# Smaller batches of moves in the transfer queue, and one of four weight sums made by adding transfers, in a stack of nine fp32 transformer stages

## The chip, the cores and the metric

One core of a Trainium2 chip runs the whole program. The metric is the device time of one execution in microseconds (us), the median of several runs. A profiled execution gives the rows that are read here; its own time and its span are given below.

## The reference, cut to what matters

The input is x, 512 tokens by 1024 features, in fp32. Nine stages follow each other: FFN stages 1, 3, 4, 6, 7 and 9, and mixers 2 (pooling and latent attention), 5 (gated convolution) and 8 (Fourier mixing and grouped attention). The change is in the FFN stages alone:

```python
def rms_norm(x, g):
    y = xf * lax.rsqrt(jnp.mean(xf * xf, axis=-1, keepdims=True) + NORM_EPS)
    return (y * g).astype(x.dtype)

def swiglu(x, w_gate, w_up, w_down):
    return (jax.nn.silu(x @ w_gate) * (x @ w_up)) @ w_down

x = x + 0.5 * swiglu(rms_norm(x, ffn_norm), w_gate, w_up, w_down)
```

w_gate and w_up are 1024 x 2816 (2752 in stages 7 and 9), w_down is 2816 x 1024.

## The kernel before, in words

**Precision.** Every fp32 operand is split in a high part (rounded to fp32r, by ACT) and a low part (the rest, by DVE). A product is three matmuls (L556 low by high, L558, L560 high by high; `mm3`). A weight block of 128 x 1024 numbers comes from HBM into one of eight `raw` slots (issued by SP, L2529), is split by ACT into `wh` (L1146, `high`) and by DVE into `wl` (L1614, `low`), and is then a *unit* that TensorE uses (12 matmuls in a group, 24 in the down projection's first part). The split buffers are a ring of four: ACT may write unit n when TensorE is through with unit n - 4. ACT and DVE work three units ahead of TensorE (two in the down projection).

**The group.** An FFN stage treats the first 2560 hidden columns in five groups of 512 (g = 0 to 4). The two products with w_gate and w_up, halved in the inner dimension and in the tokens, are a 2 x 2 block product, and it is made with seven block products instead of eight (a Strassen form). It needs four sums of activation blocks (Sf 0 to 3, made once in a stage) and four sums of weight blocks in every group, each in two halves kh = 0 and 1: t1 from B12 and B11, t2 from B22 and t1, t3 from t2 and B11, t4 from B21 and t2. So a group has 14 units, in this order: B11 (product A), t1 (E), t2 (B), t3 (D), t4 (B2), B21 (A2), B22 (E2), each twice. t1 overwrites the raw slot of B12, t3 that of B11; t2 and t4 stand in the two buffers `part`. All eight sums are made by DVE (L1601, `add`), in group 0 just before the split of their unit and in groups 1 to 4 two units earlier (`sums_before`).

TensorE leaves products A, B, D and E in PSUM; DVE combines them through U2, U3 and H (L1624: `U2`, `C22`, `C21`, `last_sum`), ACT applies silu (L1219, L1226), DVE gates (L1627).

**Turning H.** The hidden block comes out with tokens on the partitions and is needed with hidden columns there. DVE turns 32 x 32 pieces (L1717, `turn_squares`), into rows of H that are not used yet (`squares(m)`; for m = 3 into `squares3`), and sixteen transfers of 64 KB inside SBUF, issued by SP (L2536, `move_blocks`), put the 32-row pieces in their places. Groups 0 to 3 (m = 0 to 3) go that way; group 4 is turned by TensorE (L680). The last columns behind 2560 (256, or 192 in stages 7 and 9) stand in `Hrest` and are batch m = 4: turned by `turn_rest_squares` (L1724) in group 1, into rows 14 and 15 of H. H, once moved, is split into `Hh` (ACT, L1177) and `Hl` (DVE, L1624) for the down projection.

**The order of SP's queue.** SP works strictly in order. It issues the weight loads, each of which waits until its raw slot has been split for the last time (L2522), and the moves, which wait for the squares. Where the moves stand is worked out when the program is built (L2540 to L2546): a batch (q, g, u) is put ahead of the first load whose slot is released at unit u of group g or later, the whole batch of sixteen in one piece. Batches 0 and 4 are placed at units 7 and 8 of group 1, 1 and 2 at unit 7 of groups 2 and 3, and 3 at unit 10 of group 4. In stage 1 this puts batch 0 ahead of load 24 and batch 4 ahead of load 25; loads 21 to 28 are the eight of group 2, and load 25 (B22, kh = 0) is the first that t2 needs. Batch 3 stands ahead of the second down load in stage 1 and ahead of the first in the other stages, whose raw slots come free later.

POOL has little to do: in an FFN stage one power for the norm (`norm`, L2373).

Of the kernel before, what the change touches and what calls it, by code (L numbers as in the profile page):

```python
# [160 lines left out]
def plan(stream):  # L161


    loads, units, release = [], [], []
    begins = {}
    holder, ring = {}, {}
    free_at = {r: -1.0 for r in range(N_RAW)}
    sums = {}

    def load(chunk, allowed, last):  # L170
        r = min(allowed, key=lambda slot: (free_at[slot], slot))
        loads.append(Load(*chunk, r, holder.get(r)))
        holder[r], free_at[r] = len(loads) - 1, last
        release.append(last)
        return len(loads) - 1

    def unit(width, nk, allowed, ahead, source, total=None):
        r = min(allowed, key=lambda slot: (ring.get(slot, -1), slot))
        units.append(Unit(width, nk, r, ring.get(r), ahead, source, total))
        ring[r] = len(units) - 1  # L180

    for c in stream:
        u = len(units)
        if not isinstance(c[2], dict):
            n = load(c, PLAIN if u >= len(FIRST) else range(N_RAW), u)
            unit(c[1], c[2], PLAIN, 2, ("raw", n))
            continue
        s, first, blocks = c
        begins.setdefault(s, []).append(u)
        if first and s in AFTER_MIXER:  # L190
            for r in range(len(PLAIN), N_RAW):
                holder[r], free_at[r] = ("end", s - 1), u - 4.0
        raw = {}
        for name, kh in (sorted(LOADS, key=lambda part: UNITS.index(part[0]) if part[0] in UNITS[0:1] else LAST_USE[part[0]])
                         if first else LOADS):
            last = u + LAST_USE[name] + kh + (2 if first and name == "B12" else 0)
            raw[name, kh] = load(blocks[name, kh], range(N_RAW), last)
        for name in UNITS:
            for kh in range(2):
                b11, b12, b21, b22 = (("raw", raw[b, kh]) for b in ("B11", "B12", "B21", "B22"))  # L200
                part = ("part", kh)
                source, total = {
                    "t1": (b12, (b12, b11, ALU.subtract)), "t2": (part, (b22, b12, ALU.subtract)),
                    "t3": (b11, (part, b11, ALU.subtract)), "t4": (part, (b21, part, ALU.subtract)),
                    "B11": (b11, None), "B22": (b22, None), "B21": (b21, None)}[name]
                if total:
                    sums.setdefault(len(units) - (1 if first else 2), []).append(len(units))
                unit(512, 2, range(N_RING), 3, source, total)
    return loads, units, release, sums, begins

# [39 lines left out]
def build(nc, a, out):  # L250
    ctx = ExitStack()
    with ctx:
# [17 lines left out]
        par_in, gain_in, out_in = Event(sem("par_in")), Event(sem("gain_in")), Event(sem("out_in"))  # L270
        x_in = [Event(sem(f"x_in{t}")) for t in range(KT)]
        turned_in = [Event(sem(f"turned_in{q}")) for q in range(5)]

# [16 lines left out]
        sq_at = -(-(place[0] - 128) // 256) * 256 + 128  # L290
        sq = [sb(f"sq{i}", [128, T], F) for i in range(2)]
        acc = [sb(f"acc{i}", [128, T], F) for i in range(2)]
        diag_at = place[0]
# [15 lines left out]

        ident = col("ident", 0, 128)  # L310
        loads, units, release, sums_before, begins = plan(weight_stream(a))


# [11 lines left out]
        Sl = [at(f"Sl{j}", [128, 4, 256], R, 49152 + 8192 * j) for j in range(4)]  # L325
        part = [at(f"part{j}", [128, CAP], F, 77824 + 4096 * j) for j in range(2)]
        wh.append(at("wh3", [128, CAP], R, 86016))
        wl.append(at("wl3", [128, CAP], R, 90112))
# [8 lines left out]

        squares3 = at("squares3", [128, 4, 4, 128], F, 45056 + 16384)

        def squares(q):  # L340

            return squares3[:, :, :, :] if q == 3 else H[:, 4 * q + 8:4 * q + 12, :, :]

        def block_moves(s, m):

            spans = [slice(32 * i, 32 * i + 32) for i in range(4)]
            for j in spans:
                for i in spans:
                    if m < 4:
                        yield H[j, 4 * m:4 * m + 4, :, i], squares(m)[i, :, :, j]  # L350
                    else:
                        whole = (FFN[s][0] - GROUPED - j.start + 127) // 128
                        yield H[j, 20:20 + whole, :, i], H[i, 14:14 + whole, :, j]

# [774 lines left out]
        def scalar_program(e, w):  # L1129
# [3 lines left out]
            def high():  # L1133
# [4 lines left out]
                split[0] += 1  # L1138
                if units[n].sum:
                    w.wait_ge(dve, ("t", n))  # L1140
                else:
                    i = units[n].source[1]
                    w.wait_ge(raw_in[loads[i].slot], ("w", i))
# [442 lines left out]
        def vector_program(e, w):  # L1586
# [122 lines left out]
            def turn_squares(s, m, *ks):  # L1709

                w.wait_ge(dve, ("h", s, m))
                if m == 1:
                    w.wait_ge(turned_in[4], ("turned", s, 4))
                if m == 3:
                    w.wait_ge(mm, ("E", s, 4))
                for k in ks:
                    e.transpose(squares(m)[:, k, :, :], H[:, 4 * m + k, :, :]).then_inc(dve.up(("squares", s, m)), 1)  # L1717

            def turn_rest_squares(s, n):

                w.wait_ge(dve, ("h", s, 5))
                for k, cols in ((14, 128), (15, n - 128)):
                    at0 = 128 * (k - 14)
                    e.transpose(H[:, k, :, 0:cols], Hrest[:, :, at0:at0 + cols]).then_inc(dve.up(("squares", s, 4)), 1)  # L1724

# [18 lines left out]
            def last_sum(s, g):  # L1744
                x = pairs[pairs_of(s)[3]]
                w.wait_ge(mm, ("E2", s, g))
                tt(hidden(g, 0), blocks(x), blocks(U2), ALU.add, ("C12", s, g), ("read", ("E2", s, g)))

# [6 lines left out]
            def ffn(s):  # L1755
# [4 lines left out]
                w.wait_ge(act, ("second half", s))  # L1760
                tt(Sf[2][:, :, :], Qf[1][:, :, :], Sf[2][:, :, :], ALU.add, ("S1", s))
                use()
# [11 lines left out]
                for g in range(5):  # L1774
                    for u in range(14):
# [6 lines left out]
                        if u == 8:  # L1782
# [4 lines left out]
                            w.wait_ge(dve, ("U3", s, g))  # L1787
                            for m in {2: (0,), 3: (1, 4), 4: (2,)}.get(g, ()):
                                w.wait_ge(turned_in[m], ("turned", s, m))
                            tt(hidden(g, 2), blocks(x), blocks(U3), ALU.add, ("C22", s, g), ("read", ("E", s, g)))  # L1790
                        if u == 10:
# [12 lines left out]
                        if u == 3 and g == 0:  # L1804
                            w.wait_ge(act, ("other half", s))
                            w.wait_ge(dve, ("N2", s))
                            tt(Sf[3][:, :, :], Qf[2][:, :, :], Sf[1][:, :, :], ALU.add, ("S4", s))
                        if u == 5 and g == 0:
# [4 lines left out]
                        if u in (5, 6) and g == 4:  # L1813
                            turn_squares(s, 3, 2 * u - 10, 2 * u - 9)
                        if u == 4 and g == 1:
                            turn_rest_squares(s, f - GROUPED)
# [552 lines left out]
        def gpsimd_program(e, w):  # L2369
            pool.n = 0  # L2370

            def tt(dst, a, b, op, *names):
# [6 lines left out]
            def inverse_root(dst, src, shape, name, source):  # L2379
# [6 lines left out]
                w.wait_ge(pool, "half")  # L2386
                tt(dst, src, h, ALU.pow, name)

            def norm(s):
# [117 lines left out]
            for s in range(1, 10):  # L2507
                {2: mixer_mla, 5: mixer_conv, 8: mixer_fnet}.get(s, norm)(s)
                pool.also(("end", s))
# [5 lines left out]
        def sync_program(e, w):  # L2515
# [16 lines left out]

            def move_blocks(s, m):
                w.wait_ge(dve, ("squares", s, m))
                for dst, src in block_moves(s, m):
                    e.dma_start(dst, src).then_inc(turned_in[m].sem, 16)  # L2536
                    turned_in[m].n += 16
                turned_in[m].also(("turned", s, m))

            moves_before = {}  # L2540
            for s in FFN:
                for q, g, u in ((0, 1, 7), (4, 1, 8), (1, 2, 7), (2, 3, 7), (3, 4, 10)):
                    u += begins[s][g]
                    later = (n for n, load in enumerate(loads) if load.before is not None and (
                        load.before == ("end", s) if not isinstance(load.before, int) else release[load.before] >= u))
                    moves_before.setdefault(next(later, len(loads)), []).append((u, s, q))  # L2546

# [18 lines left out]
            e.dma_start(par[:, :], a["par"]).then_inc(par_in.sem, 16)  # L2566
            for n in range(13, len(loads) + 1):
                for _, s, q in sorted(moves_before.get(n, ())):
                    move_blocks(s, q)
                if n < len(loads):  # L2570
                    fetch(n)
            for part, (q0, q1) in enumerate(HALVES):
# [120 lines left out]
```

## Time and profile before

| | |
|---|---|
| median of 3 runs | 2636.38 us (2634.23 to 2637.41) |
| profiled execution | 2630.94 us |
| its span | 2629.1 us |
| TensorE (PE) busy | 2553.9 us, 97% |
| VectorE (DVE) busy | 1928.6 us, 73% |
| ScalarE (ACT) busy | 1173.5 us, 45% |
| GpSimd (POOL) busy | 136.5 us, 5% |
| mean granted TensorE clock | 0.992 |
| transfers on queue q1, share of 16 DMA engines | 37.0% |

Times in the rows count from the span's start. "Idle before" is the time that an instruction's engine stood still ahead of it, with what ended that. SPq are transfers that SP issues: the time there is the issuing, not the transfer.

### The profile page before, as it was taken

To read this page: it belongs to the slowest core of one execution; us is meant where nothing else is said; L and a number is where in the kernel's file an instruction comes from. 1 tells how busy PE (TensorE), PEld (TensorE's weight loads), DVE (VectorE), ACT (ScalarE), POOL (GpSimd) and SP (SyncE) were. 2 spreads that over 40 slices of the span, in tenths; PEclk is the share of its full clock that TensorE was granted. 3 is DMA by queue.
4 is the path that set the end of the run, shared out by engine and by line. 5 is a ranking of instruction groups with operands and counts; after the bars stand their busy time and mean duration, and the time that the engine had idled before them with its cause. 6 is when DMAs were issued, how large, how long until landed. Compare 5 with 4: busy or idle time off the path is not lost.

```text
span 2629.1 us, 31692 instructions
## 1 busy us (share of the span) xinstructions
PE 2553.9 (97%) x11743; PEld 2116.6 (81%) x11743; DVE 1928.6 (73%) x2371; ACT 1173.5 (45%) x1611; POOL 136.5 (5%) x133
## 2 busy tenths in 40 slices
PE   8999999999999999999999999999999999999998
PEld 6788888877878887788888877888787888877787
DVE  7898358888983498854556988449985479798843
ACT  6445226664443444432225544335444337644431
POOL 0000004500000000000000000000000044100000
PEclk9999999999999999999999999999999999999999
DMA  5553332134533345433333454243533321244422
GB/s 178 132 144 85 95 89 79 33 121 128 136 92 94 119 108 141 112 97 97 96 96 114 116 144 111 87 134 98 150 94 107 96 87 41 88 114 136 116 89 81
DMA packets 448761, 280.92 MB, mean 107 GB/s; under 512 B 235744, under 2 KB 383968, under 8 KB 448608
## 3 DMA queue, kind: packets, MB, share of 16 engines
q1 hardware_dynamic: 448608, 278.89, 37.0%
q8 instruction: 95, 1.56, 0.2%
q14 instruction: 58, 0.48, 0.1%
HBM read 248.68 MB, written 2.10 MB: 95 GB/s over the span
## 4 chain that ended last, share of the span: by engine, by line
PE 70%; DVE 14%; SPq 6%; issue 5%; ACT 3%; DMA 2%; DVEq 0%; POOLq 0%; POOL 0%; ACTq 0%
PE pair L556 23%; PE pair L558 22%; PE pair L560 22%; SPq L2536 5%; DVE wl L1614 5%; ACT wh L1146 1%; DMA raw<-in_ffn_w_up 1%; DMA raw<-in_ffn_w_down 1%; DVE part L1601 1%; DVE H L1717 1%; DVE U L1624 1%; PE pair L780 1%; DVE raw L1601 1%; DVE H L1627 1%; DVE squares L1717 1%
## 5 line engine op out<-in xcount | busy, mean ns | idle before, releaser
L1614 DVE TENSOR_TENSOR wl<-raw,wh 128x1024 fp32r<-128x1024 f32 (+2 forms) x547 | 647.0, 1188 | 445.0 <-ACT wh L1146 442.4
L1146 ACT ACTIVATE wh<-raw 128x1024 fp32r<-128x1024 f32 (+2 forms) x547 | 562.7, 1030 | 823.5 <-PE pair L560 749.0
L556 PE MATMUL pair<-Hh,wl 128*128 128x512 f32 (+1 forms) x1061 | 413.6, 390 | 16.7 <-DVE Hl L1624 15.7
L558 PE MATMUL pair<-Hl,wh 128*128 128x512 f32 (+1 forms) x1061 | 414.6, 391 | 0.0
L560 PE MATMUL pair<-Hh,wh 128*128 128x512 f32 (+1 forms) x1061 | 412.2, 388 | 0.0
L556 PE MATMUL pair<-wh,Sl 128*128 128x512 f32 x960 | 379.4, 395 | 25.7 <-DVE H L1624 17.7
L556 PE MATMUL pair<-wh,Xl 128*128 128x512 f32 (+2 forms) x976 | 376.3, 386 | 16.6 <-DVE wl L1614 7.0
L558 PE MATMUL pair<-wl,Sh 128*128 128x512 f32 x960 | 377.3, 393 | 0.0
L560 PE MATMUL pair<-wh,Sh 128*128 128x512 f32 x960 | 377.0, 393 | 0.0
L558 PE MATMUL pair<-wl,Xh 128*128 128x512 f32 (+2 forms) x976 | 374.1, 383 | 0.0
L560 PE MATMUL pair<-wh,Xh 128*128 128x512 f32 (+2 forms) x976 | 374.0, 383 | 0.0
L556 PEld LDWEIGHTS pair<-Hh,wl 128*128 128x128 f32 x1061 | 200.4, 189 | 60.4 <-ACT Hh L1177 17.7
L556 PEld LDWEIGHTS pair<-wh,Sl 128*128 128x128 f32 x960 | 182.5, 190 | 72.4 <-DVE H L1624 20.2
L558 PEld LDWEIGHTS pair<-Hl,wh 128*128 128x128 f32 x1061 | 200.5, 189 | 41.7
L560 PEld LDWEIGHTS pair<-Hh,wh 128*128 128x128 f32 x1061 | 200.7, 189 | 40.2
L556 PEld LDWEIGHTS pair<-wh,Xl 128*128 128x128 f32 x976 | 184.0, 189 | 55.9 <-DVE U L1624 8.8
L1146 ACT ACTIVATE wh<-part 128x1024 fp32r<-128x1024 f32 x120 | 127.4, 1062 | 225.3 <-DVE part L1601 131.7
L560 PEld LDWEIGHTS pair<-wh,Sh 128*128 128x128 f32 x960 | 182.5, 190 | 38.5
L558 PEld LDWEIGHTS pair<-wl,Sh 128*128 128x128 f32 x960 | 182.4, 190 | 37.5
L560 PEld LDWEIGHTS pair<-wh,Xh 128*128 128x128 f32 x976 | 184.1, 189 | 34.9
L558 PEld LDWEIGHTS pair<-wl,Xh 128*128 128x128 f32 x976 | 184.1, 189 | 33.9
L556 PE MATMUL pair<-Xh,wl 128*128 128x512 f32 (+1 forms) x432 | 170.9, 396 | 2.2 <-DVE Xl L1624 1.6
(325 smaller groups left out, 3287.5 us busy)
## 6 DMA issues: line engine op xcount, KB each, us to landing
raw<-in_ffn_w_gate SPq DMA_DIRECT2D x120, 512.0 KB, 4.9
raw<-in_ffn_w_up SPq DMA_DIRECT2D x120, 512.0 KB, 4.3
raw<-in_ffn_w_down SPq DMA_DIRECT2D x114, 512.0 KB, 3.5
H<-H SPq DMA_DIRECT2D x288, 64.0 KB, 2.1
raw<-in_c_w_in SPq DMA_DIRECT2D x24, 512.0 KB, 3.8
H<-squares SPq DMA_DIRECT2D x96, 64.0 KB, 2.1
raw<-in_w_in SPq DMA_DIRECT2D x10, 512.0 KB, 3.9
raw<-in_a_w_in SPq DMA_DIRECT2D x8, 512.0 KB, 3.8
```

The source lines that it names most:

```text
L556: e.matmul(o, ll, rh, start=start, stop=False, skip_group_check=again)
L558: e.matmul(o, lh, rl, start=False, stop=False, skip_group_check=again)
L560: i = e.matmul(o, lh, rh, start=False, stop=stop, skip_group_check=again)
L780: e.transpose(bank[0:rows, t * 128:(t + 1) * 128], src, ident).then_inc(mm.up(name), 1)
L1146: e.activation(part_of(n, wh), source_of(n), ACT.Copy).then_inc(whi.up(("w", n)), 1)
L1601: e.tensor_tensor(half_of(units[n].source), half_of(a), half_of(b), op).then_inc(dve.up(("t", n)), 1)
L1614: e.tensor_tensor(part_of(n, wl), source_of(n), part_of(n, wh).bitcast(F), ALU.subtract).then_inc(wlo.up(("w", n)), 1)
L1624: e.tensor_tensor(dst, a, b, op).then_inc(dve.up(*names), 1)
L1627: e.scalar_tensor_tensor(dst, a, scalar, b, op0, op1).then_inc(dve.up(*names), 1)
L1717: e.transpose(squares(m)[:, k, :, :], H[:, 4 * m + k, :, :]).then_inc(dve.up(("squares", s, m)), 1)
L2536: e.dma_start(dst, src).then_inc(turned_in[m].sem, 16)
```

## The change

Three things are changed, all in the FFN stages.

1. SP's moves of batches 0, 1 and 2 are issued in two eights, each ahead of a load: batch g - 1 ahead of the fifth load of group g + 1 and ahead of the first load behind that group's eight. Batches 3 and 4 are one sequence of 32 moves, of which 12, 2, 2, 2, 4, 4 and 6 stand ahead of the first seven down loads.
2. The last columns (batch 4) are turned in group 4, at u = 9, into a place of their own (`squares4`, over `acc`), not in group 1 into rows of H.
3. The signs in the scheme are changed so that t4 = B21 + t2 (t1 = B12 + B11, t2 = B22 + t1; S1, S4, C12 and C22 change their sign to match). DVE's instruction for t4 goes, sixty in all. In its place POOL issues a transfer from the raw slot of B21 into `part` that adds to what stands there (`accum_op`), 512 KB each. It waits for the raw block, for both splits of t2 (unit n - 4) and for t3's sum (unit n - 2). ACT's split of t4 waits for the transfer.

```diff
@@ -186,7 +186,7 @@
         s, first, blocks = c
-        begins.setdefault(s, []).append(u)
+        group_loads.setdefault(s, []).append(len(loads))
         if first and s in AFTER_MIXER:
@@ -200,13 +200,15 @@
                 source, total = {
-                    "t1": (b12, (b12, b11, ALU.subtract)), "t2": (part, (b22, b12, ALU.subtract)),
-                    "t3": (b11, (part, b11, ALU.subtract)), "t4": (part, (b21, part, ALU.subtract)),
+                    "t1": (b12, (b12, b11, ALU.add)), "t2": (part, (b22, b12, ALU.add)),
+                    "t3": (b11, (part, b11, ALU.subtract)), "t4": (part, (b21, part, None)),
                     "B11": (b11, None), "B22": (b22, None), "B21": (b21, None)}[name]
-                if total:
+                if name == "t4":
+                    adds.setdefault(s, []).append(len(units))
+                elif total:
                     sums.setdefault(len(units) - (1 if first else 2), []).append(len(units))
                 unit(512, 2, range(N_RING), 3, source, total)
-    return loads, units, release, sums, begins
+    return loads, units, release, sums, adds, group_loads
@@ -336,10 +341,11 @@
         squares3 = at("squares3", [128, 4, 4, 128], F, 45056 + 16384)
-
-        def squares(q):
-
-            return squares3[:, :, :, :] if q == 3 else H[:, 4 * q + 8:4 * q + 12, :, :]
+        squares4 = nc.alloc_sbuf_tensor_at("squares4", [128, 2, 4, 128], F, offset=acc_at)
+
+        def squares(m):
+
+            return {3: squares3, 4: squares4}[m][:, :, :, :] if m > 2 else H[:, 4 * m + 8:4 * m + 12, :, :]
@@ -350,7 +356,7 @@
                         whole = (FFN[s][0] - GROUPED - j.start + 127) // 128
-                        yield H[j, 20:20 + whole, :, i], H[i, 14:14 + whole, :, j]
+                        yield H[j, 20:20 + whole, :, i], squares4[i, 0:whole, :, j]
@@ -1136,7 +1142,9 @@
                 split[0] += 1
-                if units[n].sum:
+                if units[n].sum and units[n].sum[2] is None:
+                    w.wait_ge(added[n % 2], ("t", n))
+                elif units[n].sum:
                     w.wait_ge(dve, ("t", n))
@@ -1709,8 +1717,6 @@
                 w.wait_ge(dve, ("h", s, m))
-                if m == 1:
-                    w.wait_ge(turned_in[4], ("turned", s, 4))
                 if m == 3:
@@ -1719,9 +1725,9 @@
                 w.wait_ge(dve, ("h", s, 5))
-                for k, cols in ((14, 128), (15, n - 128)):
-                    at0 = 128 * (k - 14)
-                    e.transpose(H[:, k, :, 0:cols], Hrest[:, :, at0:at0 + cols]).then_inc(dve.up(("squares", s, 4)), 1)
+                for k, cols in ((0, 128), (1, n - 128)):
+                    e.transpose(squares4[:, k, :, 0:cols], Hrest[:, :, 128 * k:128 * k + cols]).then_inc(
+                        dve.up(("squares", s, 4)), 1)
@@ -1785,9 +1791,9 @@
                             w.wait_ge(dve, ("U3", s, g))
-                            for m in {2: (0,), 3: (1, 4), 4: (2,)}.get(g, ()):
+                            for m in {2: (0,), 3: (1,), 4: (2,)}.get(g, ()):
                                 w.wait_ge(turned_in[m], ("turned", s, m))
-                            tt(hidden(g, 2), blocks(x), blocks(U3), ALU.add, ("C22", s, g), ("read", ("E", s, g)))
+                            tt(hidden(g, 2), blocks(x), blocks(U3), ALU.subtract, ("C22", s, g), ("read", ("E", s, g)))
                         if u == 10:
@@ -1812,7 +1818,7 @@
                             turn_squares(s, 3, 2 * u - 10, 2 * u - 9)
-                        if u == 4 and g == 1:
+                        if u == 9 and g == 4:
                             turn_rest_squares(s, f - GROUPED)
@@ -2385,6 +2393,22 @@
                 tt(dst, src, h, ALU.pow, name)
+
+            def add_weights(n):
+
+                (_, b21), (_, kh), _ = units[n].sum
+                w.wait_ge(raw_in[loads[b21].slot], ("w", b21))
+                w.wait_ge(whi, ("w", n - 4))
+                w.wait_ge(wlo, ("w", n - 4))
+                w.wait_ge(dve, ("t", n - 2))
+                e.dma_start(totals[kh][:, :], raw[loads[b21].slot][:, :], accum_op=ALU.add).then_inc(added[n % 2].sem, 16)
+                added[n % 2].n += 16
+                added[n % 2].also(("t", n))
+
+            def ffn(s):
+                norm(s)
+                for n in adds[s]:
+                    add_weights(n)
@@ -2505,7 +2529,7 @@
             for s in range(1, 10):
-                {2: mixer_mla, 5: mixer_conv, 8: mixer_fnet}.get(s, norm)(s)
+                {2: mixer_mla, 5: mixer_conv, 8: mixer_fnet}.get(s, ffn)(s)
                 pool.also(("end", s))
@@ -2530,20 +2554,28 @@
-            def move_blocks(s, m):
+            def moves(s, m):
+
                 w.wait_ge(dve, ("squares", s, m))
                     turned_in[m].n += 16
-                turned_in[m].also(("turned", s, m))
+                    turned_in[m].also(("turned", s, m))
+                    yield
+
+            def last_moves(s):
+                yield from moves(s, 3)
+                yield from moves(s, 4)
             for s in FFN:
-                for q, g, u in ((0, 1, 7), (4, 1, 8), (1, 2, 7), (2, 3, 7), (3, 4, 10)):
-                    u += begins[s][g]
-                    later = (n for n, load in enumerate(loads) if load.before is not None and (
-                        load.before == ("end", s) if not isinstance(load.before, int) else release[load.before] >= u))
-                    moves_before.setdefault(next(later, len(loads)), []).append((u, s, q))
+                for g in (1, 2, 3):
+                    batch = moves(s, g - 1)
+                    for n in (4, 8):
+                        moves_before.setdefault(group_loads[s][g + 1] + n, []).append((batch, 8))
+                batch = last_moves(s)
+                for n, count in enumerate((12, 2, 2, 2, 4, 4, 6)):
+                    moves_before.setdefault(group_loads[s][4] + 8 + n, []).append((batch, count))
@@ -2564,11 +2596,11 @@
             e.dma_start(par[:, :], a["par"]).then_inc(par_in.sem, 16)
-            for n in range(13, len(loads) + 1):
-                for _, s, q in sorted(moves_before.get(n, ())):
-                    move_blocks(s, q)
-                if n < len(loads):
-                    fetch(n)
+            for n in range(13, len(loads)):
+                for batch, count in moves_before.get(n, ()):
+                    for _ in range(count):
+                        next(batch)
+                fetch(n)
             for part, (q0, q1) in enumerate(HALVES):
```

Left out are the places where a name is set up or passed on, and three more of the changed signs.

## Rows read from the trace of the kernel before

**Rows 1.** The page, part 1: busy us, share, instructions.
```profile
PE 2553.9 (97%) x11743; PEld 2116.6 (81%) x11743; DVE 1928.6 (73%) x2371; ACT 1173.5 (45%) x1611; POOL 136.5 (5%) x133
```

**Rows 2.** TensorE's waits: us in total, times, longest us.
```profile
PE pair L556 <- DVE H L1624: 17.7, 6, 4.7
PE pair L556 <- DVE Hl L1624: 15.7, 5, 4.2
PE pair L556 <- DVE wl L1614: 15.1, 17, 7.0
PE pair L556 <- DVE U L1624: 5.4, 4, 1.4
```

**Rows 3.** Timeline of TensorE, stage 3, group 2: start us, us, [idle before].
```profile
673.85 0.39 PE L556 MATMUL pair<-wh,Xl 128*128 128x512 f32 x1
674.07 0.39 PE L558 MATMUL pair<-wl,Xh 128*128 128x512 f32 x1
```

**Rows 4.** Timeline of SP's queue, stage 1, group 1.
```profile
93.08 12.05 SPq L2536 DMA_DIRECT2D H<-H  x16
...
105.85 11.94 SPq L2536 DMA_DIRECT2D H<-H  x16
117.89 1.05 SPq L2529 DMA_DIRECT2D raw<-in_ffn_w_up  x2
```

**Rows 5.** Timeline of DVE, the same stretch.
```profile
91.75 1.30 DVE L1717 STREAM_TRANSPOSE H<-H 128x512 f32<-128x512 f32 x2
...
100.02 1.22 DVE L1614 TENSOR_TENSOR wl<-raw,wh 128x1024 fp32r<-128x1024 f32 x1
...
122.21 1.22 DVE L1601 TENSOR_TENSOR part<-raw,raw 128x1024 f32<-128x1024 f32 x1 [7.78 <-DMA raw<-in_ffn_w_up]
```

**Rows 6.** Timeline of TensorE at the start of group 2, stage 1.
```profile
125.76 0.79 PE L556 MATMUL pair<-wh,Sl 128*128 128x512 f32 x1 [4.70 <-DVE H L1624]
```

**Rows 7.** Timeline of SP's queue, end of stage 3's groups.
```profile
749.12 11.97 SPq L2536 DMA_DIRECT2D H<-squares  x16
761.20 37.70 SPq L2529 DMA_DIRECT2D raw<-in_ffn_w_down  x10
```

**Rows 8.** Timeline of ACT, the same stretch.
```profile
765.53 1.06 ACT L1146 ACTIVATE wh<-raw 128x1024 fp32r<-128x1024 f32 x1 [7.29 <-DMA raw<-in_ffn_w_down]
...
767.64 1.05 ACT L1146 ACTIVATE wh<-raw 128x1024 fp32r<-128x1024 f32 x1
```

**Rows 9.** Timeline of TensorE, stage 3: group 0, and the down projection's start.
```profile
591.87 0.50 PE L556 MATMUL pair<-wh,Xl 128*128 128x512 f32 x1 [1.32 <-DVE U L1624]
...
770.70 0.61 PE L556 MATMUL pair<-Hh,wl 128*128 128x512 f32 x1 [4.21 <-DVE Hl L1624]
```

**Rows 10.** Windows: PE, PEld, DVE, ACT, POOL busy (count), PE clock, DMA share, GB/s.
```profile
125.70:129.70 4.00, 3.94 (x10) 3.17 (x11) 3.86 (x6) 1.06 (x1) 0.00 (x0) 0.57 0.53 139
...
2380.40:2384.40 4.00, 3.93 (x12) 3.19 (x13) 3.86 (x6) 1.06 (x1) 0.00 (x0) 0.69 0.60 142
...
591.80:595.80 4.00, 3.93 (x17) 3.27 (x18) 3.97 (x5) 0.81 (x1) 0.00 (x0) 1.00 0.13 15
...
770.70:774.70 4.00, 4.00 (x11) 3.17 (x12) 4.00 (x6) 2.57 (x5) 0.00 (x0) 0.57 0.56 171
...
2494.60:2498.60 4.00, 3.90 (x10) 3.15 (x11) 4.00 (x6) 2.68 (x5) 0.00 (x0) 0.57 0.54 181
```

**Rows 11.** The page, part 6: transfers, KB each, us from issue to landing.
```profile
raw<-in_ffn_w_gate SPq DMA_DIRECT2D x120, 512.0 KB, 4.9
...
H<-H SPq DMA_DIRECT2D x288, 64.0 KB, 2.1
```

**Rows 12.** Groups of DVE: count | busy us, mean ns | idle before.
```profile
L1601 DVE TENSOR_TENSOR part<-raw,part 128x1024 f32<-128x1024 f32 x60 | 73.4, 1224 | 4.4
```

**Rows 13.** Timeline of DVE, stage 3, group 0.
```profile
577.79 1.23 DVE L1601 TENSOR_TENSOR raw<-part,raw 128x1024 f32<-128x1024 f32 x1
```

**Rows 14.** Timeline of DVE, stage 3, group 2.
```profile
660.03 1.22 DVE L1614 TENSOR_TENSOR wl<-part,wh 128x1024 fp32r<-128x1024 f32 x1
```

More of the change, by code:

```diff
@@ L164, in plan @@
     loads, units, release = [], [], []
-    begins = {}
+    group_loads = {}
     holder, ring = {}, {}
     free_at = {r: -1.0 for r in range(N_RAW)}
-    sums = {}
+    sums, adds = {}, {}
     def load(chunk, allowed, last):
@@ L271, in build @@
         x_in = [Event(sem(f"x_in{t}")) for t in range(KT)]
+        added = [Event(sem(f"added{i}")) for i in range(2)]
         turned_in = [Event(sem(f"turned_in{q}")) for q in range(5)]
@@ L291, in build @@
         sq = [sb(f"sq{i}", [128, T], F) for i in range(2)]
+        acc_at = -(-(place[0] - 128) // 256) * 256 + 128
         acc = [sb(f"acc{i}", [128, T], F) for i in range(2)]
@@ L310, in build @@
         ident = col("ident", 0, 128)
-        loads, units, release, sums_before, begins = plan(weight_stream(a))
+        loads, units, release, sums_before, adds, group_loads = plan(weight_stream(a))
         stage_at = -(-(stage_base - 128) // 256) * 256 + 128
@@ L326, in build @@
         part = [at(f"part{j}", [128, CAP], F, 77824 + 4096 * j) for j in range(2)]
+        totals = part
         wh.append(at("wh3", [128, CAP], R, 86016))
@@ L1746, in last_sum @@
                 w.wait_ge(mm, ("E2", s, g))
-                tt(hidden(g, 0), blocks(x), blocks(U2), ALU.add, ("C12", s, g), ("read", ("E2", s, g)))
+                tt(hidden(g, 0), blocks(x), blocks(U2), ALU.subtract, ("C12", s, g), ("read", ("E2", s, g)))
             def hidden(g, first):
@@ L1760, in ffn @@
                 w.wait_ge(act, ("second half", s))
-                tt(Sf[2][:, :, :], Qf[1][:, :, :], Sf[2][:, :, :], ALU.add, ("S1", s))
+                tt(Sf[2][:, :, :], Qf[1][:, :, :], Sf[2][:, :, :], ALU.subtract, ("S1", s))
                 use()
@@ L1806, in ffn @@
                             w.wait_ge(dve, ("N2", s))
-                            tt(Sf[3][:, :, :], Qf[2][:, :, :], Sf[1][:, :, :], ALU.add, ("S4", s))
+                            tt(Sf[3][:, :, :], Qf[2][:, :, :], Sf[1][:, :, :], ALU.subtract, ("S4", s))
                         if u == 5 and g == 0:
@@ L2370, in gpsimd_program @@
             pool.n = 0
+            for event in added:
+                event.n = 0
             def tt(dst, a, b, op, *names):
```

## The prediction, made before the result was known

> **What bounds the kernel now.** I read the page first, for the shares: TensorE is busy for 97% of the span [rows 1], so only the stretches in which it stands still can be won. The view of waits gives these by what ended them [rows 2]: 17.7 us in six waits for DVE's H, 15.7 us in five for Hl, 15.1 us in 17 for wl (one of 7.0 us at the start), 5.4 us in four for U. Then I followed each kind back through the timelines. Matmuls start 0.22 to 0.23 us apart and are drawn 0.39 us long [rows 3], so a wait costs 0.16 us more than its printed idle time.
>
> The first kind stands at the start of group 2 of every FFN stage. In stage 1 SP issues sixteen moves in 12.05 us, one load, then sixteen more in 11.94 us, and only at 117.89 us the next two loads [rows 4]. DVE has stood still for 7.78 us when the first of them has landed, and makes its sum at 122.21 us [rows 5]. TensorE gets its buffer (the H wait) after 4.70 us [rows 6]. The second kind stands at the start of the down projection: SP issues sixteen moves in 11.97 us and only then, at 761.20 us, the first down loads [rows 7]; ACT splits the first at 765.53 us after 7.29 us of waiting for it [rows 8]; TensorE waits 4.21 us for Hl [rows 9]. The engine that sets these stalls is SP's queue.
>
> **The clock is part of the price.** After the stall at 125.7 us the granted clock over 4 us is 0.57, after that at 2380.4 us 0.69; these are the first and the last of six stalls of the first kind, and all six have such a dip (I take the mean of both, 0.63). With levels 2.4 and 1.2 GHz, a window of 4 us at mean clock c loses 4(1 - c): 1.72 and 1.24 us. Of the five Hl stalls three have one, the first and the last of them at 1.72 us [rows 10].
>
> **Part 1: moves in eights (gain 30 us).** Removed: both blocks of sixteen ahead of the loads of group 2. The batch of the last columns leaves group 1 altogether, and the other batch is split, eight moves, four loads, eight moves. Moves take 12.05/16 = 0.75 us each [rows 4], so eight hold SP for 6.0 us. In stage 1 the squares are turned by 93.05 us (two transposes from 91.75 us) and the load that DVE later misses has its slot free at 101.24 us, when the split that began at 100.02 us ends [rows 5]. In the new order SP issues the load before it, then eight moves, done by about 102 us, then this load, which lands some 4.9 us later [rows 11], at 107 us. DVE wanted it at 122.21 - 7.78 = 114.4 us: 7 us of cover. The second eight stand behind three further loads, which have their slots by then. So the stall goes: 17.7 + 6 x 0.16 = 18.7 us; the dips, six at a mean of 1.48, 8.9 us; and the six short wl waits that follow some 15 us later, where DVE is still catching up. The 16 wl waits other than the longest hold 8.1 us [rows 2], so 0.5 + 0.16 each, 4 us. Together 31.6; I take 30. The bounds are 15 (half of it comes back as shorter waits) and 32. What is late next is nothing that I can find: later groups already have one batch of sixteen ahead of loads and no stall.
>
> **Part 2: last group (gain 17 us).** The last columns are turned in group 4 (two transposes, 1.3 us like those of [rows 5]; DVE waits 7 us for the down load there, which covers them). SP issues twelve moves ahead of the first down load, not sixteen; then 2, 2, 2, 4, 4 and 6 between the loads. Twelve of 11.97/16 = 0.75 us are four fewer: the first down load is 3.0 us earlier in stage 3 [rows 7]. The blocks of the other stages last 10.68 to 11.32 us, so 2.7 to 2.8 us there. The second load comes 0.56 + 1.5 us behind the first, at 760.3 us instead of 761.8, and lands at about 764.6 us, if it takes the 4.3 us of the first (761.20 to 765.53). ACT needs it behind its first split and two silus (765.53 to 767.64 us in [rows 8], 3 us earlier in the new order, 764.6 us). So it is just in time; the third load, at 762.3 us, is level with before, and its values are wanted later. The waits shrink by 2.7 to 3.0 us in five stages: 13.9 us, which leaves 1.4 us in stage 3 and next to nothing in three. The dips behind three of them (1.72 + 1.24 + 1.72, the middle one in stage 6) are 4.7 us; a wait of 1.32 us elsewhere is followed by a clock of 1.00 [rows 9, 10]. In all 18.6 us; I take 17. Stage 1 is its own case: its first down load came before the moves and now comes behind twelve, at 228 us, which costs its 1.1 us wait nothing either way. Lower bound 5 us: the pairs of moves between loads give the gain back on the second load.
>
> **Part 3: sixty sums leave DVE (gain 7 us).** 60 instructions of 1.224 us are 73.4 us of DVE [rows 12], but where DVE waits for ACT anyway this buys nothing. It buys where DVE is the bound: in group 0. There U2 is done 2 sums (2.3 us) late, and TensorE waits 1.32 us for it in stage 3 [rows 9]. The four U waits are 5.4 + 4 x 0.16 = 6.0 us, and in stages 1 and 9 a wl wait behind the first sum goes (0.6 + 0.16 each): 7.5 us; I take 7. Other bound 0, if the add comes no earlier than the sum did. The changed signs alter no instruction's size.
>
> **Part 4: sixty adding transfers (price 0).** Behind POOL's waits stands only the next add: its own work in an FFN stage is one small power at the start. Who waits is ACT's split, then DVE's. The room: in group 0 of stage 3 the third sum starts at 577.79 us and is done 1.22 us later [rows 13], so the first add can start at 579.0. TensorE is ready for the product at 591.87 - 1.32 - 0.16 = 590.4 us [rows 9], and a split of 1.06 on ACT and 1.22 on DVE takes 2.4 us with hand-over. So the transfer has 590.4 - 2.4 - 579.0 = 9.0 us, its twin (third sum done 3.5 us later, product 2.7 us later) 8.2 us. In group 2 the last reader of the buffer starts at 660.03 us and takes 1.22, and the product starts at 673.85 us: 673.85 - 2.4 - 661.25 = 10.2 us [rows 3, 14]. The trace has no transfer from POOL and none that adds. The nearest rows are a 64 KB move inside SBUF, 2.1 us to landing, and a 512 KB load, 4.9 us [rows 11]. The ends I take are 2.1 us and 9.8 us (two passes of 4.9, as it must read two operands). I take 6: one such pass and a microsecond for POOL. At 6 us nothing waits; at 9.8 us group 0 loses 0.8 + 0.8 us in six stages, 10 us with ACT's own delays counted not at all. Sixty transfers of 4.9 us on the sixteen queues add under 300 us of a resource that is 37% busy; I give nothing for it, since the loads now have 7 us of cover.
>
> The Trainium skill speaks both ways here. Its page DMA: Bandwidth & Descriptors, "Anatomy of one DMA", fits 2.0 us + bytes/436e3 for a transfer issued from GpSimd: an estimate of 3.2 us for 512 KB, and the sum would stay. Its page SBUF, "A bandwidth-pool intuition that's wrong", tells of such a transfer at 3.1 us instead of 0.62 beside a DVE copy, because GpSimd can't write its descriptors. Estimated by that the add would be 8.5 us, and the sum 2 us less; no run here shows it yet.
>
> **Sum.** 30 + 17 + 7 - 0 = 54 us. The profiled execution took 2630.9 us (span 2629.1), so 2577 of its kind; the median of the three runs is 2636.4, 5.4 above it, and my time goes by that: 2582 us.
>
> **Rivals.**
> (a) Forecast, all stalls of the first kind gone, those of the second cut: 2574 to 2598 us. Chance 0.62.
> (b) The last group gives nothing: the down projection starts as late because the second and third load stand behind pairs of moves, or the wait passes to ACT. The exact fit above (764.6 against 764.6 us) speaks for it, the four moves fewer against. 2636 - 30 - 7 = 2599 us. Chance 0.13.
> (c) The adds land at about 9 to 10 us: group 0 gains nothing (7) and loses 10, ACT in its order holds up the copy of U behind it, and some dips stay (5): 2582 + 22 = 2604 us. Chance 0.10.
> (d) Slower: the adds take longer than the room. Each then holds ACT, and with it TensorE, by what is over. With x us each the loss is 24 (x - 10.2) + 6 (x - 8.2), for one wait per group, and it eats the 54 us at x = 11.6; at x = 13 it is 96 us, so 2636 + 42 = 2678 us. Against it: twice the slowest row is 9.8 us. For it: nothing measured, and in group 0 DVE works without a gap, should that hold POOL up. Chance 0.11.
> (e) The moves' stall is replaced by another wait of DVE of equal length, or the cuts don't come about: 2632 to 2640 us. Chance 0.04.
>
> **Numbers.** No change means within 0.2%, 5 us, about what a measurement of this kernel can tell. Faster: 0.62 + 0.13 + 0.10 = 0.85; same 0.04; slower 0.11. The range of 8 in 10 takes in (a) to (c) with an edge: 2570 to 2612 us.
>
> **What would show it.** SP: blocks of eight of about 6 us, and between 93 and 118 us of stage 1 at least five loads. DVE: no wait for in_ffn_w_up in group 1. TensorE: H waits gone, Hl waits at most 1.5 us, U waits gone, the clock dips behind all these stalls gone but one or two. POOL: sixty issues; time from issue to landing under 8 us, and ACT's waits for part no longer than before. Wrong if ACT's splits of part wait for the transfer by more than 8 us, or if TensorE's Hl waits stay above 2.5 us.

## The result, and the profile after

The changed kernel takes 2590.24 us (median of 4 runs, 2583.78 to 2590.74) against 2635.31 us for the kernel before beside it: 45 us less, a ratio of 0.9823 with a 95% interval of 0.9806 to 0.9841. The forecast was 2582 us, 54 us less, in a range of 2570 to 2612.

The page of the profile after (span 2588.5 us, execution 2590.34 us), parts 1 and 6; the first row stands against [rows 1], the others against [rows 11]:

```profile
PE 2539.8 (98%) x11743; PEld 2111.6 (82%) x11743; DVE 1864.9 (72%) x2311; ACT 1174.7 (45%) x1611; POOL 189.2 (7%) x193
...
part<-raw POOLq DMA_DIRECT2D x60, 512.0 KB, 5.8
H<-H SPq DMA_DIRECT2D x288, 64.0 KB, 3.7
```

DVE has its sixty instructions less, POOL issues sixty transfers, which land 5.8 us after issue in the median, and the moves of batches 0 to 2, which now run beside loads and adding transfers, need 3.7 us, not 2.1. What TensorE waits for, after, against [rows 2]:

```profile
PE pair L562 <- DVE wl L1622: 11.3, 9, 7.3
PE pair L562 <- DVE Hl L1632: 11.1, 5, 3.0
PE pair L562 <- DVE U L1632: 2.6, 2, 2.0
...
PE pair L562 <- ACT onesR L1185: 1.9, 1, 1.9
```

The six waits for H are gone altogether (17.7 us). The waits for U fell from 5.4 to 2.6 us. The five for Hl fell only from 15.7 to 11.1 us, and that of stage 1, named onesR because ACT copies constants there, rose from 1.0 to 1.9.

I added up, over TensorE's timeline, by how much each start is later than 0.227 us behind the one before, which takes in the slow clock. Start of group 2 in six stages with what follows it: 32.7 us before, nothing after. Start of the down projection in six stages: 23.0 before, 19.3 after. Group 0: 15.5 before, 12.8 after, 2.7 us less. The program's first 14 us: 1.3 less. Together 40 us of the 40.6 by which the span fell.

SP's queue in stage 1, group 1, after, against [rows 4]:

```profile
94.45 7.65 SPq L2561 DMA_DIRECT2D H<-H  x8
102.20 3.03 SPq L2553 DMA_DIRECT2D raw<-in_ffn_w_up  x2
```

The load that t2 needs is issued at 102.20 us, not at 117.89; DVE makes the sum at 115.44 us without waiting for it. Then the down projection's start in stage 6: SP's queue, and under it ACT's splits and TensorE's first matmul.

```profile
1590.88 7.97 SPq L2561 DMA_DIRECT2D H<-squares  x12
1598.95 0.57 SPq L2553 DMA_DIRECT2D raw<-in_ffn_w_down  x1
1599.56 1.27 SPq L2561 DMA_DIRECT2D H<-squares  x2
1600.93 0.56 SPq L2553 DMA_DIRECT2D raw<-in_ffn_w_down  x1
```
```profile
1603.56 1.06 ACT L1154 ACTIVATE wh<-raw 128x1024 fp32r<-128x1024 f32 x1 [2.79 <-DMA raw<-in_ffn_w_down]
...
1607.08 1.06 ACT L1154 ACTIVATE wh<-raw 128x1024 fp32r<-128x1024 f32 x1 [1.31 <-DMA raw<-in_ffn_w_down]
```
```profile
1610.14 0.47 PE L562 MATMUL pair<-Hh,wl 128*128 128x512 f32 x1 [1.90 <-DVE Hl L1632]
```

The first load is split 4.6 us after its issue, and ACT then waits for the second, split 6.15 us after its issue. The same three steps before, in the same stage: SP's queue, ACT, TensorE.

```profile
1616.41 10.68 SPq L2536 DMA_DIRECT2D H<-squares  x16
1627.19 6.77 SPq L2529 DMA_DIRECT2D raw<-in_ffn_w_down  x4
```
```profile
1631.20 1.06 ACT L1146 ACTIVATE wh<-raw 128x1024 fp32r<-128x1024 f32 x1 [5.66 <-DMA raw<-in_ffn_w_down]
...
1633.30 1.05 ACT L1146 ACTIVATE wh<-raw 128x1024 fp32r<-128x1024 f32 x1
```
```profile
1636.36 0.47 PE L556 MATMUL pair<-Hh,wl 128*128 128x512 f32 x1 [2.58 <-DVE Hl L1624]
```

Counted from the first move: first load 10.78 us before and 8.07 after (2.7 earlier, as forecast), first split 14.79 and 12.68 (2.1 earlier), second split 16.89 and 16.20 (0.7 earlier), first matmul 19.95 and 19.26 (0.7 earlier). The gain is lost at the second load. Stage 6 is no exception: from its issue to its landing the second load takes 6.1 to 6.5 us in all six stages after, and 4.8 to 5.3 before.

### The profile page after: what moved, and what is told of

Read it like the earlier page. It is cut to its first block, busy times and chain, and to the rows that moved or that the text cites. A ratio compares the mean times of both kernels' runs of the same rounds, so it can differ in the third digit from the quotient of the medians.

```text
span 2588.5 us, 31758 instructions
## 1 busy us (share of the span) xinstructions
PE 2539.8 (98%) x11743; PEld 2111.6 (82%) x11743; DVE 1864.9 (72%) x2311; ACT 1174.7 (45%) x1611; POOL 189.2 (7%) x193
## 4 chain that ended last, share of the span: by engine, by line
PE 86%; DVE 6%; ACT 2%; SPq 2%; DMA 2%; issue 1%; DVEq 0%; POOLq 0%; POOL 0%; ACTq 0%
PE pair L562 28%; PE pair L566 27%; PE pair L564 27%; SPq L2561 2%; DVE wl L1622 1%; DMA raw<-in_ffn_w_down 1%; ACT wh L1154 1%; PE pair L786 1%; DMA part<-raw 1%; DVE Xl L1632 0%; DVE squares L1723 0%; PE pair L686 0%; PE pair L862 0%; PE pair L861 0%; DVE X L1632 0%
## 5 line engine op out<-in xcount | busy, mean ns | idle before, releaser
L562 PE MATMUL pair<-Hh,wl 128*128 128x512 f32 (+1 forms) x1061 | 413.4, 390 | 13.0 <-DVE Hl L1632 11.1
L562 PE MATMUL pair<-wh,Sl 128*128 128x512 f32 x960 | 374.2, 390 | 4.0 <-DVE wl L1622 4.0
```

What stands on the lines that cost most here:

```text
L562: e.matmul(o, ll, rh, start=start, stop=False, skip_group_check=again)
```

## The experiments

**1. The sums back on VectorE, SP's order kept.**

```diff
-"t4": (part, (b21, part, None))
+"t4": (part, (b21, part, ALU.add))     # by DVE, no transfer from POOL
```

> The changed kernel with the sixty t4 sums back on VectorE (t4 = B21 + t2 by DVE; SP's order of moves kept). Theory (the gain is SP's order, and the adds trade 7 us of expected gain for about 2): in the profile of the changed kernel group 0 is 1.6 us better in stage 3, 1.5 in stage 7, 1.7 in stage 9 and 2.5 worse in stage 1, so undoing costs about 2 us: profiled time 2590 to 2595, U waits of 1.3 us back in stages 3 and 7, H waits at the start of group 2 still absent, the Hl waits of the last group unchanged at 1.9 to 3.0 us. Rival (DVE's relief is what took the H waits away): H waits of 1 us or more come back at the start of group 2 in six stages, time 2605 or more.

2590.52 us (5 runs, 2588.04 to 2594.36), ratio 0.9842 (0.9829 to 0.9856). TensorE's waits:

```profile
PE pair L560 <- DVE Hl L1630: 9.2, 5, 2.5
PE pair L560 <- DVE U L1630: 5.5, 4, 1.5
```

No wait for H, Hl waits somewhat shorter, U waits back to four. The theory holds in its main point: the H waits go by SP's order, without relief for DVE. That nothing at all is lost against the changed kernel is not shown. Its 2590.24 us were measured beside another set of runs of before; by the ratios (0.9842 here, 0.9823 and 0.9827 in its two sets) it is 4 to 5 us better, within the intervals. And the profile shows two effects that cancel. Added up as above, group 0 is late by 16.2 us, much as before (15.5), and not by 12.8; but the down projection's start is late by 14.7 us, not 19.3, because only one clock dip follows it (three in the changed kernel) and one of the Hl waits is only 0.6 us long.

**2. The adding transfers alone, SP's order of before.** The old placing of sixteens, and the last columns turned in group 1.

> The kernel before with the adding transfers alone: SP's moves in sixteens at their old places, last columns turned in group 1, t4 by POOL's transfers. Theory (SP's order is the gain): H waits of 2.3 to 4.7 us at the start of group 2 stay in all six stages with their clock dips, time 2626 to 2637, that is 0 to 9 us below before. Rival (DVE's relief matters there): H waits shrink by 1 us or more each, time under 2620.

2626.06 us (6 runs), ratio 0.9973 (0.9961 to 0.9985): 7 us below before.

```profile
PE pair L562 <- DVE H L1632: 21.6, 6, 5.4
PE pair L562 <- DVE Hl L1632: 15.6, 5, 4.0
PE pair L562 <- DVE wl L1622: 11.2, 10, 6.6
...
PE pair L562 <- DVE U L1632: 2.6, 2, 2.0
```

The H waits stay; they even grow by 3.9 us, and the clock dips behind five of them stay. The wl and U waits fall by 6.7 us together. Added up as above, group 2 comes out even (32.7 us before, 33.0 here) and group 0 gains 4 (15.5 and 11.3). That is the adds' own effect: a few microseconds.

**3. The first three down loads together.**

```diff
-for n, count in enumerate((12, 2, 2, 2, 4, 4, 6)):
+for n, count in enumerate((12, 0, 0, 6, 4, 4, 6)):
```

> The changed kernel with the last group's moves in 12, 0, 0, 6, 4, 4, 6 instead of 12, 2, 2, 2, 4, 4, 6: the first three down loads stand together behind twelve moves. Theory A (the moves between the first down loads delay the second load, by 1.3 us of issue and by sharing the transfer engines; it lands 6.2 us after its issue): the first load lands 4.2 us after its issue as before, the second is no longer waited for, Hl waits fall from about 2.0 to under 0.8 us in stages 3, 6, 7, 9, clock dips behind them go, time 2572 to 2582. Theory B (the start is bound by the splits, silus and Hh on ACT behind the first load alone, and the backlog of twelve moves holds the first load): Hl waits stay at 1.5 us or more, time 2586 to 2592.

2571.27 us (4 runs, 2570.52 to 2574.32), ratio 0.9768 (0.9755 to 0.9781). Theory A. Stage 6, SP's queue and ACT:

```profile
1580.91 7.98 SPq L2561 DMA_DIRECT2D H<-squares  x12
1588.98 2.01 SPq L2553 DMA_DIRECT2D raw<-in_ffn_w_down  x3
```
```profile
1593.14 1.06 ACT L1154 ACTIVATE wh<-raw 128x1024 fp32r<-128x1024 f32 x1 [2.35 <-DMA raw<-in_ffn_w_down]
...
1595.24 1.05 ACT L1154 ACTIVATE wh<-raw 128x1024 fp32r<-128x1024 f32 x1
```

The first load is split 4.16 us after its issue (4.6 in the changed kernel) and the second without a wait. The waits at the down projection are 0.0 to 0.6 us in all six stages, and no clock dip follows them. The second load, issued 0.66 us behind the first and not 1.97, lands in 5.0 to 5.5 us in the six stages, not 6.1 to 6.5. Added up as above, the down projection's start is late by 3.2 us, not 19.3: 16 us. The medians say the same, each against the runs of before beside it: 61 us below before here, 45 in the changed kernel.

**4. A pair of loads behind nine moves**, at the time at which their slots come free: counts 9, 0, 4, 3, 4, 6, 6.

> The changed kernel with the last group's moves in 9, 0, 4, 3, 4, 6, 6: two down loads together behind nine moves, at the time at which their slots come free. Theory A: first load 2 us earlier and second with it; Hl waits gone in all six stages (under 0.4 us), no clock dip behind them, time 2570 to 2578, that is 12 to 20 us below the changed kernel. Theory B (the loads' landing does not matter, something else holds Hl): no change, 2586 to 2592.

2571.4 us (4 runs, 2569.76 to 2571.77), ratio 0.9765 (0.9752 to 0.9778). All six waits are down to 0.2 us, yet the time is that of the last experiment: once the wait is next to nothing, an earlier load buys nothing.

```profile
PE pair L562 <- DVE Hl L1632: 1.3, 6, 0.2
```

**5. The same moves with less data.** Batch 3 carries one block in four, so three quarters of that batch are not turned.

```diff
-yield H[j, 4 * m:4 * m + 4, :, i], squares(m)[i, :, :, j]
+n = 1 if m == 3 else 4
+yield H[j, 4 * m:4 * m + n, :, i], squares(m)[i, 0:n, :, j]
```

> The changed kernel in which the sixteen moves of batch 3 in the last group carry one of their four blocks (16 KB, not 64 KB); three quarters of that batch are not turned. Theory (the first down load is held by the issuing of twelve moves, the second load by issue and by sharing): if the moves' data is part of it, the first load lands in 4.0 to 4.3 us, not 4.6 to 5.2, and the second, whose neighbours are half light moves, in 5 to 5.5 us, not 6.2; Hl waits fall by about 1 us or more each. If it is issuing alone and issuing costs the same for a light move, nothing changes. If a light move is issued faster, the first load comes earlier by that.

2573.02 us (2 runs), ratio 0.9771 (0.9751 to 0.9790). Stage 6, SP's queue and ACT:

```profile
1583.32 7.66 SPq L2562 DMA_DIRECT2D H<-squares  x12
1591.09 0.54 SPq L2554 DMA_DIRECT2D raw<-in_ffn_w_down  x1
...
1593.23 0.54 SPq L2554 DMA_DIRECT2D raw<-in_ffn_w_down  x1
```
```profile
1595.12 1.06 ACT L1155 ACTIVATE wh<-raw 128x1024 fp32r<-128x1024 f32 x1 [1.91 <-DMA raw<-in_ffn_w_down]
...
1597.65 1.06 ACT L1155 ACTIVATE wh<-raw 128x1024 fp32r<-128x1024 f32 x1 [0.32 <-DMA raw<-in_ffn_w_down]
```

Twelve light moves are issued in 7.66 us, twelve whole ones in 7.97: issuing costs nearly the same. The order is that of the changed kernel. But the first load is split 4.0 us after its issue (4.6) and the second after 4.4 (6.15); over the six stages the second lands in 4.0 to 4.7 us, not 6.1 to 6.5, and sooner than the 5 to 5.5 that I had expected. So what the moves transfer beside the loads holds them, 1.7 us in the case of the second load, and that is more than the 1.3 us for which the pair holds the queue. A light move has a quarter of the bytes and also a quarter of the separate 128-byte pieces (128, not 512); which of the two counts is not shown.

**6. Sixteens again, the last columns still in group 4.** Next to it the changed kernel once more.

```diff
-for n in (4, 8):
-    moves_before.setdefault(group_loads[s][g + 1] + n, []).append((batch, 8))
+moves_before.setdefault(group_loads[s][g + 1] + 4, []).append((moves(s, g - 1), 16))
```

> The changed kernel with batches 0, 1 and 2 in one piece of sixteen ahead of the fifth load of the next group (batch 4 still in group 4). Theory (what made the H waits was two batches of sixteen with one load between them, so taking batch 4 out of group 1 is enough): sixteen moves from about 95 to 107 us in stage 1, the load that t2 needs lands at 112 to 113 us where DVE wants it at 114; no H wait over 0.5 us, time within 4 us of the changed kernel. Rival (the cut in eights is what helps): H waits of 1 to 2 us in six stages with some clock dips, 8 to 20 us slower than the changed kernel.

> The changed kernel once more, beside the next three, to compare them on one chip: 2584 to 2592 us.

2587.43 us (4 runs) beside 2588.04 us (4 runs); ratios 0.9827 (0.9812 to 0.9841) and 0.9827 (0.9813 to 0.9842). SP's queue, stage 1, group 1:

```profile
94.50 12.38 SPq L2561 DMA_DIRECT2D H<-H  x16
106.99 1.07 SPq L2553 DMA_DIRECT2D raw<-in_ffn_w_up  x2
```

No wait for H. The cut in eights does nothing here; that batch 4 no longer stands in group 1, so that sixteen moves and not 32 are ahead of the load that t2 needs, does it all.

**7. The adds made late.** Three sums on a scratch tile on GpSimd ahead of each.

```diff
+for _ in range(3):
+    e.tensor_tensor(idle[:, :], half[:, 0:4], half[:, 4:8], ALU.add).then_inc(pool.up(), 1)
+    w.wait_ge(pool, HERE)
 e.dma_start(totals[kh][:, :], raw[loads[b21].slot][:, :], accum_op=ALU.add)...
```

> The changed kernel with three small sums on a scratch tile on GpSimd ahead of each adding transfer, so that each add is some 2 to 3 us later and the second of a pair some 5 us. Theory (there is room of about 10 us in groups 1 to 4 and of 6.7 us in group 0, where U2 stands behind the split of t4 in VectorE's order; an add now takes 6.5 us from ready to landed): group 0 loses 2 to 4 us in each of six stages and groups 1 to 4 up to 1.5 us each, in all 20 to 60 us slower than the changed kernel; GpSimd's waits shrink. Rival (ACT's waits for part are already on the path): 3 to 5 us are lost per group, 90 us or more. Rival (the room is wider still): under 10 us.

2672.55 us (4 runs), 84 us above the changed kernel beside it, ratio to before 1.0151 (1.0134 to 1.0168). I had 20 to 60, and the rival 90 or more; neither was met. POOL, ACT and TensorE in stage 1, group 2, three views:

```profile
133.07 0.89 POOL L2408 DMA_DIRECT2D part<-raw  x1 [0.30 <-POOL idle L2406]
...
135.74 0.87 POOL L2408 DMA_DIRECT2D part<-raw  x1 [0.38 <-POOL idle L2406]
```
```profile
138.23 1.06 ACT L1155 ACTIVATE wh<-part 128x1024 fp32r<-128x1024 f32 x1 [5.75 <-DMA part<-raw]
...
143.87 1.06 ACT L1155 ACTIVATE wh<-part 128x1024 fp32r<-128x1024 f32 x1 [4.58 <-DMA part<-raw]
```
```profile
146.34 0.47 PE L563 MATMUL pair<-wh,Xl 128*128 128x512 f32 x1 [1.41 <-DVE wl L1623]
```

The first of the pair lands 5.2 us after its issue, the second, issued while the first is under way, 8.1 us. The second is the one that decides: its third sum is done at 131.3 us, it lands at 143.87, 12.6 us later, and TensorE loses 1.6 us (the 1.41 of the row and the 0.16 that a printed idle time leaves out). Room is therefore 11.0 us there, and the changed kernel, with 8.0 us in the median, is 3 us within it. Added up as above and against the profile of the changed kernel beside it, groups 1 to 4 lose 38 us (1.6 each), group 0 loses 24, clock dips included, and the start of the down projection 23: in group 4 the squares are turned behind the late splits in DVE's order, so the last moves and down loads are late too. The first move is issued 17.0 us ahead of the group's last matmul in the changed kernel and 13.9 to 15.5 us ahead here. That third item I had not counted.

**8. With the last group mended, are the adds worth anything?** The order of experiment 4 with sums on VectorE, and with adding transfers once more.

> The changed kernel with the last group in 9, 0, 4, 3, 4, 6, 6 and the sixty t4 sums back on VectorE. Theory (with the Hl waits gone the adds are worth what they save in group 0 of stages 3, 7 and 9, some 2 to 5 us): 2571 to 2577 us against 2571 for the same order with adding transfers; U waits of 1.3 us in stages 3 and 7. Rival (the adds cost transfer time that the loads miss): this version is faster, 2566 to 2570 us.

> The order 9, 0, 4, 3, 4, 6, 6 with adding transfers once more, beside the version with sums on VectorE: 2569 to 2573 us.

2576.33 us (4 runs, 2575.60 to 2577.53) against 2571.78 us (5 runs, 2570.01 to 2573.11): ratios to before 0.9779 (0.9766 to 0.9792) and 0.9759 (0.9746 to 0.9773). The adds are worth 4 to 5 us; the two sets of runs don't overlap, though the intervals of the ratios do. In the profiles nearly all of it is in group 0, late by 16.7 us and by 12.7. The U waits show a part of it: with sums on VectorE, then with adding transfers,

```profile
PE pair L560 <- DVE U L1630: 5.4, 4, 1.5
```
```profile
PE pair L562 <- DVE U L1632: 2.6, 2, 2.0
```

The best versions are thus the orders of experiments 3 and 4 with adding transfers, not to be told apart: 2571 to 2572 us in three sets of runs. Each taken against before beside it, that is 16 to 18 us below the changed kernel.

## Why the prediction came out 8 us too low

The 8 us flatter the parts. In the profiles the gain is 40.6 us where the sum had 54, so 13 us are missing: part 1 gave 3 more than its term, part 2 gave 13 less, part 3 gave 4 less, and 1 came at the program's start. The profiled execution of before was 5.4 us faster than the median from which the forecast started, and that of the changed kernel is at its median. That this hides 5 of the 13 us is luck.

**What bounds the kernel: right.** SP's queue made both kinds of stall, as experiments 1 and 2 show from both sides for the H waits, and 3 and 4 for the Hl waits.

**Part 1, 30 us: right in size (32.7), partly wrong in its reason.** The waits, the short wl waits behind them and the clock dips went together. But the gain was written to "moves in eights", and experiment 6 shows that eights are not needed. My own sum could have shown it: sixteen moves from 95 us end at 107, and the load then lands at 112, before the 114.4 us at which DVE asks. That eight moves took 0.96 us each here and not 0.75 (7.65 us for eight, [rows 4] for sixteen) cost nothing, because of the 7 us of cover.

**Part 2, 17 us: the term that was mis-sized; it gave 3.7 us.** The step "the first down load is 3.0 us earlier" held (2.7 in stage 6). The step that failed is "if it takes the 4.3 us of the first": I gave the second load the landing time of a load with no moves behind it. It took 6.1 to 6.5 us, since the moves put between the loads are transferred beside it (experiment 5), on top of their issuing, which I had counted (1.5 us, it took 1.3). The first load took 4.6 to 6.0 us as well, where it had taken 4.0 to 4.3 in these five stages. Even with no move beside it the second load of a pair took more than 4.3: 4.8 to 5.3 us before and 5.0 to 5.5 in experiment 3. This is rival (b)'s mechanism, "the second and third load stand behind pairs of moves", to which I had given 0.13 although I noted that the fit was exact. As the waits stayed at 1.9 to 3.0 us, three clock dips stayed as well, priced at 4.7 us. My own sign of being wrong, an Hl wait above 2.5 us, came true in stage 4 (3.0). And stage 1, where I had said that twelve moves ahead of its first down load cost nothing, waits 1.9 us and not 1.0. Removing the pairs gave another 16 us (experiments 3 and 4), so that the last group in all gave 20 us where part 2 had promised 17.

**Part 3, 7 us: 2.7 in the profile, 4 to 5 by experiment 8.** The U waits of stages 3 and 7 went and stage 9 gained 1.7 us, but stage 1 lost 2.5. Some 1.7 of that is a clock dip behind its U wait (granted clock 0.58 over 4 us), which the second profile of the same kernel does not have; there group 0 is late by 10.4 us, 5 less than before. The chain of waits of the changed kernel there, the longest pieces in order of time:

```profile
49.20 7.28 DMA part<-raw
...
56.51 1.07 ACT wh L1154
...
57.60 1.23 DVE wl L1622
58.83 1.14 DVE Sl L1632
59.96 1.14 DVE U L1632
...
61.15 0.50 PE pair L562
```

U2 stands behind the split of t4 in DVE's order, so the room of group 0 is not the 9.0 us up to the product but less by Sl and U2, 2.3 us: 6.7 us. From the third sum (48.6 us) to landing the transfer took 7.9 us there, and 6.4 in the median of the six stages; why it takes longer in stage 1 stays open. In stages 1 and 9 DVE has more to do in group 0 and the wait for U stays.

**Part 4, price 0 at 6 us each: close.** From issue to landing they take 4.5 to 8.9 us, 5.8 in the median, and in group 0 0.6 us more from the third sum to the issue:

```profile
L2404 POOL DMA_DIRECT2D part<-raw x60: 850/868/1058, 49.2 to 2424.7; - x60
...
DMA to landing us min/median/max: 4.5/5.8/8.9
```

The Trainium skill's page DMA: Bandwidth & Descriptors ("Anatomy of one DMA") gives an estimate of 3.2 us by its fit, which names no adding transfer; the trace has 5.8 us for an adding one, and here the measurement decides. Carried over from a DVE copy to this DVE's two-input sums and splits, the account on the Trainium skill's page SBUF ("A bandwidth-pool intuition that's wrong") gave the prediction its estimate of 8.5 us; POOL's issue took 0.87 us beside a busy DVE and the median transfer took 5.8, so the trace doesn't show such a stall here. Rival (d), slower, fell for the changed kernel, and experiment 7 shows that its mechanism is real: with adds that land 3 to 4 us later the kernel is slower than before. Put 12.6 us into its formula and it gives 24 x 2.4 + 6 x 4.4 = 84 us, which is what was measured, but by accident. The forecast counted the room of groups 1 to 4 from the end of t2's low split, which in experiment 7 is 132.4 us and not 131.3; so counted the add takes 11.4 us, and its room is 9.9, close to the 10.2 that I had. With that, and 11.3 us in group 0, the formula gives 24 x 1.2 + 6 x 3.1 = 47 us. The groups lost 62, clock dips included, and the down projection's start, which it leaves out, the rest.

## What to carry to other kernels

In a queue that issues strictly in order, look for the single load that is asked for first and count everything that stands ahead of it; taking one batch out of the way was worth 33 us, cutting the batches finer nothing. A small transfer between two loads costs the second load twice, once for its issuing (0.66 us) and once for what it transfers beside it (1.7 us for the moves of experiment 5), so put the loads that the next stage starts with side by side and the small transfers behind them. And when work is moved from an engine to a transfer, measure the room along the order of the engine that waits for it, with the instructions that stand behind the waiting one, not only up to the final reader.

## What was not expected of the hardware

A move of 64 KB takes 0.66 us to issue and one of 16 KB 0.64 us (7.97 and 7.66 us for twelve), yet the heavier ones lengthen the landing of a 512 KB load between them from 4.4 to 6.15 us. Of two adding transfers of 512 KB issued 2.7 us apart in experiment 7 the first lands after 5.2 us and the second after 8.1 us. And a clock dip (a stretch at 1.2 GHz, not 2.4) is not tied to a stall's length alone. The window behind the 2.1 us wait of stage 3 has a granted clock of 0.66, that behind the 3.0 us wait of stage 4 has 1.00; the windows of the changed kernel:

```profile
756.80:760.80 4.00, 3.95 (x12) 3.16 (x13) 4.00 (x6) 2.71 (x5) 0.00 (x0) 0.66 0.90 217
1097.70:1101.70 4.00, 3.95 (x17) 3.30 (x18) 4.00 (x6) 2.64 (x5) 0.00 (x0) 1.00 0.77 190
```

Nor does the place decide. The second profile of the same kernel has it the other way round, 1.00 behind the 2.2 us wait of stage 3 and 0.62 behind the 2.3 us wait of stage 4:

```profile
755.00:759.00 4.00, 3.99 (x18) 3.28 (x18) 4.00 (x6) 2.59 (x5) 0.00 (x0) 1.00 0.72 176
1093.70:1097.70 4.00, 4.00 (x12) 3.13 (x13) 4.00 (x6) 2.54 (x5) 0.00 (x0) 0.62 0.85 188
```

So the same wait is followed by a dip in one execution and not in another, and a dip or two, 1.7 us each, is a part of the difference between two profiles. What decides stays open.
